# A hybrid SGU/SSD/MoE layer in one kernel: gain vectors multiplied into rows before the transposes, remainders taken out of PSUM banks

## The reference

```
h  = RMSNorm(x) * mix_norm
h @ w_in -> u | v | z | xBC (2048) | dt (16) | gate_a | gate_b
yA = gelu(u) * (W_s LayerNorm(gelu(v)) + b)            # 8 heads, 128 positions
xBC -> causal depthwise conv (4 taps) -> SiLU -> xs | B | C
yB = GroupedRMSNorm(SSD(xs, dt, B, C) * SiLU(z)) * ssm_norm
x += (sigmoid(gate_a) * (yA @ Wa) + sigmoid(gate_b) * (yB @ Wb)) @ Wo
x += MoE(RMSNorm(x))          # top 4 of 32 experts, clamped SwiGLU, w1 8 MB and w2 4 MB each
x += sigmoid((RMSNorm(x) * ple_norm) @ Wg) * (p @ Wp)
out = RMSNorm(x) * final_norm
```

## Time and profile before

| | |
|---|---|
| median of three runs | 1341.76 us |
| the profiled execution's own time | 1345.77 us |
| its span, first to last instruction | 1343.7 us |
| mean granted clock of PE | 0.965 of full speed |
| PE busy | 1240.8 us, 92% |
| DVE busy | 371.2 us, 28% |
| ACT busy | 238.3 us, 18% |
| POOL busy | 189.6 us, 14%, all of it before 302 us |
| DMA | 456.63 MB, mean 340 GB/s |

### The profile page before, as it was taken

The page is one execution under the profiler, slowest core; times in us unless marked ns, Lnnn a source line. Parts: engine busy times, 40 slices in busy tenths (PEclk is TensorE's granted clock), DMA queues, the critical chain, the costliest instruction groups (busy, mean ns, idle before and its releaser), DMA issues.

```text
span 1343.7 us, 15395 instructions
## 1 busy us (share of the span) xinstructions
PE 1240.8 (92%) x6309; PEld 657.5 (49%) x6309; DVE 371.2 (28%) x672; ACT 238.3 (18%) x284; POOL 189.6 (14%) x54
## 2 busy tenths in 40 slices
PE   1998999789899999999999999999999999999976
PEld 1996888667444444444333334333333433333342
DVE  6436731542212221122121112212111221211132
ACT  4454435432000010000010000001000000100011
POOL 6555557850000000000000000000000000000000
PEclk7988999899599999999999999999999999999988
DMA  6443347757199999999999999999999999999910
GB/s 212 157 130 125 123 168 247 300 172 278 43 410 429 429 429 429 429 428 427 428 429 428 429 429 429 429 429 429 427 429 428 429 428 429 429 429 429 429 53 31
DMA packets 61094, 456.63 MB, mean 340 GB/s; under 512 B 6784, under 2 KB 16368, under 8 KB 36496
## 3 DMA queue, kind: packets, MB, share of 16 engines
q1 hardware_dynamic: 61072, 456.32, 82.6%
HBM read 455.25 MB, written 1.05 MB: 340 GB/s over the span
## 4 chain that ended last, share of the span: by engine, by line
DMA 47%; PE 45%; DVE 4%; issue 1%; ACT 1%; SPq 0%; DVEq 0%; ACTq 0%
DMA wring<-in_w_dram 45%; PE bank L810 15%; PE bank L572 5%; PE bank L573 5%; PE bank L574 5%; PE bank L840 4%; PE bank L787 3%; DVE a_lo L1166 2%; PE bank L911 2%; PE bank L796 1%; DMA blk<-in_w_in_dram 1%; DMA blk<-in_w_branch_b_dram 1%; PE bank L675 1%; PE bank L859 1%; PE bank L697 1%
## 5 line engine op out<-in xcount | busy, mean ns | idle before, releaser
L810 PE MATMUL bank<-wring,hT 128*64 128x512 f32 x2048 | 456.0, 598 | 28.7 <-DMA wring<-in_w_dram 28.7
L810 PEld LDWEIGHTS bank<-wring,hT 128*64 128x64 f32 x2048 | 140.4, 137 | 322.9 <-issue 255.7
L840 PE MATMUL bank<-wring,xbcT 128*64 128x512 f32 x1024 | 226.8, 595 | 0.0
L538 POOL TENSOR_TENSOR blk_lo<-blk,blk_hi 128x2048 fp32r<-128x2048 f32 x40 | 187.2, 4690 | 111.2 <-ACT blk_hi L924 111.0
L1467 DVE TENSOR_SCALAR xbcT<-bank 128x512 f32<-128x512 f32 x32 | 22.1, 692 | 461.8 <-PE bank L816 461.8
L840 PEld LDWEIGHTS bank<-wring,xbcT 128*64 128x64 f32 x1024 | 70.8, 137 | 152.1 <-issue 152.1
L787 PEld LDWEIGHTS bank<-xbcT,ga 128*128 128x128 f32 x1056 | 126.2, 196 | 5.1 <-issue 2.3
L787 PE MATMUL bank<-xbcT,ga 128*128 128x64 f32 x1056 | 124.9, 278 | 1.8 <-issue 1.8
L1084 ACT ACTIVATE xbcT<-xbcT 128x512 f32<-128x512 f32 x32 | 20.2, 630 | 500.3 <-DVE xbcT L1467 500.3
L924 ACT ACTIVATE blk_hi<-blk 128x2048 fp32r<-128x2048 f32 x40 | 76.4, 1913 | 122.3 <-DMA blk<-in_w_in_dram 69.7
L572 PE MATMUL bank<-blk_hi,a_lo 128*128 128x512 f32 x192 | 78.1, 407 | 14.2 <-DVE a_lo L1166 8.7
(11 more groups left out here) (228 smaller groups left out, 970.1 us busy)
## 6 DMA issues: line engine op xcount, KB each, us to landing
wring<-in_w_dram SPq DMA_DIRECT2D x192, 2048.0 KB, 21.7
blk<-in_w_in_dram SPq DMA_DIRECT2D x28, 1024.0 KB, 5.2
blk<-in_w_branch_a_dram SPq DMA_DIRECT2D x4, 1024.0 KB, 5.3
blk<-in_w_branch_b_dram SPq DMA_DIRECT2D x4, 1024.0 KB, 6.4
blk<-in_w_out_dram SPq DMA_DIRECT2D x4, 1024.0 KB, 5.1
blk<-in_w_ple_gate_dram SPq DMA_DIRECT2D x4, 1024.0 KB, 8.9
x<-in_x_dram SPq DMA_DIRECT2D x4, 512.0 KB, 5.1
v<-in_w_ple_proj_dram SPq DMA_DIRECT2D x1, 1024.0 KB, 7.5
```

Source lines behind the costliest of these rows:

```text
L538: nc.gpsimd.tensor_tensor(dst, raw, hi.bitcast(FP32), ALU.subtract).then_inc(done, 1)
L810: last = mm(bank[dh * SLOTS:(dh + 1) * SLOTS, :], xgT[:, k, :], wring[:, 2 * c + kk, off + dh * W:off + (dh + 1) * W], start=(k == 0), sto ...
L840: last = mm(YB[dh * SLOTS:(dh + 1) * SLOTS, :], actT[:, kk * P + c * SLOTS:kk * P + (c + 1) * SLOTS], wring[:, at, (kk % 2) * D + dh * W:( ...
```

## The change

- `mix_norm` and `ssm_norm` are no longer rows to be transposed with the other parameters. Each is loaded as 1024 numbers on all 128 partitions: `mix_gain` (in z's buffer) right behind x, `ssm_gain` (in the upper part of the conv buffer) after the unit `("yo", 1)` is filled.
- DVE multiplies them into the rows, ahead of the transposes, in the instruction that multiplies with the root: two of 128x1024 at the start, eight of 128x256 for the SSD branch.
- The banks of `xT` and `ybT` then hold the finished values; high and low parts of both are taken straight from the banks, like those of `yaT` and `mT`. Two of the passes through SBUF, `hT` and `ybT`, are gone there.
- The second x tile's square sum is DVE's; a dummy root on ACT comes first.
- ACT splits block 0 after the high parts of `xT`, and in two halves of 128 columns of each k (`per_k`); POOL subtracts it in two halves and PE waits for each half.
- Half block 1 is loaded ahead of the parameter rows, and PE transposes these after the first xBC block.
- ACT splits the last half block of z before the exponentials of the decays. POOL still does all 40 subtractions; their semaphore is two (`xbc_low`, `nat_low`).

```diff
@@ -78,9 +78,9 @@
     nat = lambda n: [(n, b, t) for b in range(HALVES) for t in range(TT)]
-    u = [("param",)]
-    u += [("xT", t, h) for t, h in two]
-    u += [("xbc", b, j) for b in range(4) for j in range(2)]
+    u = [("xT", t, h) for t, h in two]
+    u += [("xbc", 0, 0), ("param",)]
+    u += [("xbc", b, j) for b in range(4) for j in range(2)][1:]
     u += [("dt",)]
...
@@ -106,8 +106,9 @@
 BANKS = 8
-ROWS = {"mix": 0, "ple": 8, "ssm": 16, "sgu_b": 24, "conv_b": 32, "conv_w": 48}
-NROWS = 48 + TAPS * CONV_TILES
+ROWS = {"ple": 0, "sgu_b": 8, "conv_b": 16, "conv_w": 32}
+NROWS = 32 + TAPS * CONV_TILES
+XBC_HALVES = 8
...
@@ -209,13 +210,14 @@
-        ybT = xbcT[:, 0:KT, :]
         wpp = flat(v).rearrange("p (k n) -> p k n", k=PLE // P)
         p_nat = xc[:, 2560:3072].rearrange("p (t n) -> p t n", t=TT)
+        ssm_gain = xc[:, 3072:4096].rearrange("p (g n) -> p g n", g=GROUPS)
+        mix_gain = z[:, 0, :]
         fnorm = z[:, 0, :]
...
@@ -420,13 +427,14 @@
                 load(x[:, t, :], x_in[0, t * P:(t + 1) * P, :], x_loaded[t])
+            load(mix_gain, vec(mix_norm), mix_loaded)
             load_half(0)
-            for key, src in (("mix", rows(mix_norm)), ("ple", rows(ple_norm)),
-                             ("ssm", rows(ssm_norm)), ("sgu_b", sgu_b[0]), ("conv_b", rows(conv_b)),
+            load_half(1)
+            for key, src in (("ple", rows(ple_norm)), ("sgu_b", sgu_b[0]), ("conv_b", rows(conv_b)),
                              ("conv_w", rows(conv_w[0]))):
                 load(prow[r:r + src.shape[0], :], src, rows_loaded)
-            for i in range(1, NB):
+            for i in range(2, NB):
                 load_half(i)
...
@@ -461,6 +469,7 @@
                     wait_filled(sp, ("yo", 1))
+                    load(ssm_gain.rearrange("p g n -> p (g n)"), vec(ssm_norm), ssm_loaded)
                     load(p_nat, p_in[0, 0].rearrange("(t p) n -> p t n", p=P), p_loaded)
...
@@ -538,12 +547,17 @@
-            for i in range(SPLIT):
-                if i == HALF_OF["xbc", 3, 0]:
+            for c in range(2):
+                cols = slice(c * P, (c + 1) * P)
+                pool.wait_ge(blk_high, c + 1)
+                subtract(per_k(blk_lo[:, 0, :])[:, :, cols], per_k(blk[:, 0, :])[:, :, cols], per_k(high(0))[:, :, cols],
+                         xbc_low)
+            for i in range(1, SPLIT):
+                if i == XBC_HALVES - 2:
                     pool.wait_ge(wdt_high, 1)
                     subtract(wdt_lo[:], wdt.rearrange("p k h -> p (k h)"), wdt_hi[:], wdt_low)
-                pool.wait_ge(blk_high, i + 1)
-                subtract(blk_lo[:, i % NB, :], blk[:, i % NB, :], high(i), blk_low)
+                pool.wait_ge(blk_high, i + 2)
+                subtract(blk_lo[:, i % NB, :], blk[:, i % NB, :], high(i), xbc_low if i < XBC_HALVES else nat_low)
...
@@ -581,7 +595,7 @@
-                        pe.wait_ge(blk_low, i + 1)
+                        pe.wait_ge(nat_low, i - XBC_HALVES + 1)
                         for t in range(TT):
...
@@ -595,29 +609,30 @@
             pe.wait_ge(consts, 1)
-            pe.wait_ge(rows_loaded, 16 * 6)
-            transposes(("param",), [prow[0:NROWS, :]])
             for t in range(TT):
-            pe.wait_ge(act_low, 4)
+            wait_taken(pe, *all_of("xT"))
             for b in range(4):
                     wait_empty(pe, name)
-
-                    pe.wait_ge(blk_low, i + 1)
                     for c in range(2):
+
+                        pe.wait_ge(xbc_low, i + 2 if i else c + 1)
                         for k in range(KT):
                     last.then_inc(full(name), 1)
+                    if i == 0:
+                        pe.wait_ge(rows_loaded, 16 * 4)
+                        transposes(("param",), [prow[0:NROWS, :]])
             pe.wait_ge(wdt_low, 1)
...
@@ -728,7 +743,7 @@
-            pe.wait_ge(act_low, 8)
+            wait_taken(pe, *all_of("ybT"))
             natural("wb", a_hi, a_lo)
...
@@ -921,7 +936,12 @@
                 act.wait_ge(blk_loaded[i % NB], 16 * (i // NB + 1))
-                fn(high(i), blk[:, i % NB, :], ACT.Copy).then_inc(blk_high, 1)
+                if i == 0:
+                    for c in range(2):
+                        cols = slice(c * P, (c + 1) * P)
+                        fn(per_k(high(i))[:, :, cols], per_k(blk[:, i, :])[:, :, cols], ACT.Copy).then_inc(blk_high, 1)
+                else:
+                    fn(high(i), blk[:, i % NB, :], ACT.Copy).then_inc(blk_high, 1)
...
@@ -932,7 +952,12 @@
-            square_sums(lambda t: act.wait_ge(x_loaded[t], 16), 0, u)
+            act.wait_ge(consts, 1)
+            fn(vmean[:, 0, 0:1], ones[:, 0:1], ACT.Sqrt)
+            act.wait_ge(x_loaded[0], 16)
+            fn(u[:, 0, :], x[:, 0, :], ACT.Square, accum_out=ssq[:, 0:1]).then_inc(ssq_done, 1)
+            act.wait_ge(ms_done, 1)
+            fn(rstd[:], ssq[:], ACT.Sqrt).then_inc(rstd_done, 1)
...
@@ -952,14 +977,19 @@
+            def high_parts(kind, dst):
+
+                for t in range(TT):
+                    for h in range(2):
+                        name = (kind, t, h)
+                        wait_filled(act, name)
+                        fn(dst[:, 4 * h:4 * h + 4, t * P:(t + 1) * P], seg4(bank_of(name)[:, :]),
+                           ACT.Copy).then_inc(act_high, 1)
+
+            act.wait_ge(xn_done, TT)
+            high_parts("xT", a_hi)
             split(0)
             split(1)
-
-            for t in range(TT):
-                for h in range(2):
-                    wait_taken(act, ("xT", t, h))
-                    cols = (slice(None), slice(4 * h, 4 * h + 4), slice(t * P, (t + 1) * P))
-                    fn(a_hi[cols], hT[cols], ACT.Copy).then_inc(act_high, 1)
             split(2)
...
@@ -995,15 +1025,6 @@
-            def high_parts(kind, dst):
-
-                for t in range(TT):
-                    for h in range(2):
-                        name = (kind, t, h)
-                        wait_filled(act, name)
-                        fn(dst[:, 4 * h:4 * h + 4, t * P:(t + 1) * P], seg4(bank_of(name)[:, :]),
-                           ACT.Copy).then_inc(act_high, 1)
-
             def copy(name, dst, src=None):
...
@@ -1018,6 +1039,7 @@
             natural("u", ACT.Gelu, u)
+            split(HALF_OF["z", 1, 1])
             for c in range(TT):
...
@@ -1025,7 +1047,10 @@
             for b in range(HALVES):
-                split_ahead("z", b)
+                if b == 0:
+                    split(HALF_OF["ga", 0, 0])
+                else:
+                    split_ahead("z", b)
                 for t in range(TT):
...
@@ -1051,12 +1076,7 @@
-            wait_filled(act, ("gb", 1, 1))
-            for t in range(TT):
-                for h in range(2):
-                    wait_taken(act, ("ybT", t, h))
-                    cols = (slice(None), slice(4 * h, 4 * h + 4), slice(t * P, (t + 1) * P))
-                    fn(a_hi[cols], ybT[cols], ACT.Copy).then_inc(act_high, 1)
+            high_parts("ybT", a_hi)
             split_ahead("wa", 1)
...
@@ -1147,29 +1167,27 @@
-            norm(0, v)
-            wait_filled(dve, ("param",))
-            cp(paramT[:], bank_of(("param",))[:, 0:NROWS]).then_inc(empty(("param",)), 1)
-            wait_taken(dve, ("param",))
-            for t in range(TT):
-                for h in range(2):
-                    scaled(("xT", t, h), hT, paramT[:, ROWS["mix"]:ROWS["mix"] + KT], t, h)
-
-            def low_parts(kind, raw, hi, lo, n):
+            def low_parts(kind, hi, lo, n):
                         cols = (slice(None), slice(4 * h, 4 * h + 4), slice(t * P, (t + 1) * P))
-                        if raw is not None:
-                            tt(lo[cols], raw[cols], hi[cols].bitcast(FP32), ALU.subtract).then_inc(act_low, 1)
-                        else:
-                            name = (kind, t, h)
-                            tt(lo[cols], seg4(bank_of(name)[:, :]), hi[cols].bitcast(FP32),
-                               ALU.subtract).then_inc(empty(name), 1)
-
-            low_parts("xT", hT, a_hi, a_lo, 0)
+                        name = (kind, t, h)
+                        tt(lo[cols], seg4(bank_of(name)[:, :]), hi[cols].bitcast(FP32),
+                           ALU.subtract).then_inc(empty(name), 1)
+
+            dve.wait_ge(x_loaded[1], 16)
+            stt(u[:, 1, :], x[:, 1, :], 1.0, x[:, 1, :], ALU.mult, ALU.mult, accum_out=ssq[:, 1:2]).then_inc(ssq_done, 1)
+            norm(0, None)
+            dve.wait_ge(mix_loaded, 16)
+            for t in range(TT):
+                stt(v[:, t, :], x[:, t, :], rstd[:, t:t + 1], mix_gain, ALU.mult, ALU.mult).then_inc(xn_done, 1)
+            low_parts("xT", a_hi, a_lo, 0)
+            wait_filled(dve, ("param",))
+            cp(paramT[:], bank_of(("param",))[:, 0:NROWS]).then_inc(empty(("param",)), 1)
+            wait_taken(dve, ("param",))
...
@@ -1343,11 +1361,14 @@
             dve.wait_ge(yrstd_done, 1)
```

(24 more changed lines are left out.)

## The result

The changed kernel took 1320.47 us (median of four runs, 1319.52 to 1320.76), the kernel before 1341.28 (four runs). The ratio is 0.9842, 95% interval 0.9825 to 0.9859: 20.8 us, against a forecast of 25.8 and a time of 1316.0 within 1311 to 1324. The profiled execution took 1319.52 us, with a span of 1317.5.

A forecast was written before the change was run, and what follows sets the result against it. PE's two waits for `a_lo` were taken to bound the kernel ahead of the DMA-paced expert loop. Terms of 14.7 and 11.1 us sum to 25.8, giving 1316.0 us from the 1341.8 median, range 1311 to 1324.

The forecast's parts named there:

- first term: Start of the kernel: PE's first xBC block begins at 16.3 instead of 31.34 us, saving 14.7 us, range 10.0 to 17.0.
- A wait for `a_lo` is POOL's hold on DVE; a bank read is free of it: Low parts at both waits: about 5 us each beside GpSimd from SBUF, 2.48 us for four out of a PSUM bank.
- POOL next in line, but just covered: First blocks: GpSimd works just ahead of PE without delaying it, by 0.9 us at the tightest.
- Second term: Between "wa" and "wb": PE's 8.7 us wait for ybT's low parts and 2.4 of low clock go, 11.1 us.
- taken from both: The 25.8 us saving subtracted alike from the profiled execution, 1345.8 to 1320.0, and from the median, 1341.8 to 1316.0.
- Nothing given back by the additions: Behind "wb": DVE's additions of ga and gb end as far behind it as before, so nothing is lost.
- Edits at no time: z's last half split earlier and eight ssm multiplications, 3.6 us for 2.36: both off PE's path, no time.
- Loop moves one for one: Expert loop: its DMA stream shifts by whatever starts expert 0 earlier, with 29.37 us per expert unchanged.
- PE waited for POOL at no block but the first: Rival, 10%: GpSimd binds the first blocks at the start, giving 1322 us.
- its matmuls reached full pace: Rival, 4%: PE's clock stays at its low level through the first eight blocks, up to 45 us longer, 1361 us.
- "wb" had its weights: Rival, 8%: the weights of "wb" come late, so PE's second wait stays with another owner, 1327 us.
- the multiplications with the ssm row ended before POOL's next subtraction: Rival, 4%: DVE's ssm-row multiplications are caught by GpSimd's subtractions and delay "wa", 1322.4 us.

The follow-up runs named there:

- pool_wait: Kernel before plus one wait: GpSimd begins its weight subtractions only when the four low parts of xT are done; 1330.93 us, ratio 0.991.
- order_both: Kernel before plus two waits: GpSimd's first subtraction waits for xT's low parts, its first of wb for ybT's; 1324.70 us, ratio 0.9879.
- ybt_only: Kernel before with only the ybT part changed: ssm gain row, eight multiplications, high and low parts from the banks; 1333.67 us, ratio 0.9933.
- split_first: Kernel after, but ACT splits the first half of block 0 ahead of xT's high parts; 1318.77 us, ratio 0.9823.
- the second trace: Kernel before, unchanged, profiled once more in the first experiment; 1338.91 us, span 1336.9.
- start_only: Kernel after with the ybT part as in the kernel before, so only the start is changed; 1326.93 us, ratio 0.988.
- after_again: Kernel after, unchanged, run again beside the kernel before on one chip; 1320.35 us, ratio 0.9843.
- order_gap: Kernel before plus one wait: GpSimd's subtraction of wb's third quarter waits for the low parts of ybT; 1340.34 us, ratio 0.9993.
- whole_block: Kernel after with block 0 split and subtracted whole instead of in halves; 1322.63 us, ratio 0.9855.
- the run with 21: split_first plus 21 extra PE matmuls of 128 columns between constants at the start; 1317.26 us, ratio 0.9826.
- the run with 44: split_first plus 44 extra PE matmuls of 128 columns between constants at the start; 1321.05 us.

## Why the prediction was right, and where it was off

The forecast was a saving of 25.8 us; 20.8 came, with the time inside the range. The mechanism held at every step; the sizes of both terms were too large, the first by 1.5 us, the second by about 4 for a typical execution. The forecast for an execution like the profiled one, 1320.0, met 1319.5, and that is in part luck: the 1.5 us that the first term lacks came back behind "wb", mostly as scatter in the expert loop.

- **A wait for `a_lo` is POOL's hold on DVE; a bank read is free of it.** Right, and shown four ways: pool_wait and order_both (POOL away: 0.6 us each), ybt_only (both forms in one execution), split_first (bank reads through a subtraction).
- **First term, 14.7.** It measured 13.7 at the first block, 13.2 at dt and 12.9 at the end of "wa". The multiplications started at 8.37, not 7.3: the gain row, 6.6 us on its way, landed at 8.3 us, between the 7.0 taken and the 9.1 of the bound. ACT's high parts came 0.85 apart, at the pace of PE's transposes (four at 0.21 to 0.23), with 0.60 each instead of 0.52. Halves cost half (2.36 and 1.0), as taken. PE's first block begins at 17.61, outside the 16 to 17 named as a sign, and takes 7.8 us, 0.5 more than before.
- **POOL next in line, but just covered.** Right: five pieces back to back from 15.11 to 33.5, and no wait of PE for POOL once block 0 has begun. One sign of being wrong, over 2 us of PE waiting for POOL in the first blocks, came by its words: PE waits 4.2 us ahead of block 0. But the forecast's own layout had 4.0 there (transposes until 12.3, start at 16.3), so the sign should have named the waits behind that one. The parameter transpose cost 0.3 or less.
- **Second term, 11.1.** "wb" ends 24.1 us earlier than in the profiled trace, 11.2 more than "wa" does: near exact for that execution. It is the step that failed for the median, together with the line "taken from both". The prediction saw that its execution was 4.0 us above the median, and subtracted the whole of its wait from the median all the same. The wait is 8.7 in some executions and 4.3 in others, so the typical term is about 7. Against the second trace the same stages give 12.7 + 7.3 = 20.0 at the end of "wb", and start_only's median is 6.6 above after's. The hint was in the rows: a low part of 0.68 among ones of 5 us says that a gap let one through, and this gap depends on a load.
- **Nothing given back by the additions.** Right: the last of them ends at 272.3, 6.7 us behind "wb"; before it was 7.0 (291.85 + 4.79 against 289.67).
- **Edits at no time.** z's half: 1.4 us of waiting on DVE, 0.1 on the kernel. The ssm multiplications: 3.26 us (3.6 taken), done 1.0 us before POOL's next subtraction at 197.19.
- **Loop moves one for one.** Right: 24.7 at expert 0, 26.2 at the end, with 980.5 against 982.0 us for the loop, inside its own scatter. One expert still takes 29.37 us where DMA bounds it (606.64 to 636.01 in the chain of waits).

Of the rivals, none came: PE waited for POOL at no block but the first, its matmuls reached full pace 4.4 us into block 0 (0.21 us apart before that, 0.12 after, against 3.5 us in the kernel before), "wb" had its weights, and the multiplications with the ssm row ended before POOL's next subtraction.

## What to carry to other kernels

Where VectorE and GpSimd both stream SBUF data, look for VectorE instructions of two SBUF tensors whose length is that of a GpSimd instruction; let one operand come from PSUM, or let GpSimd wait: two semaphore waits alone gave 16 of the 21 us here. A wait that ends with another engine's instruction comes in whole instructions, so before subtracting it from a median, get a second trace or look whether a gap of a fraction of a microsecond decides it. And when a start is a chain, try each piece that an engine could do while idle: half a split put ahead of the high parts was worth about 1.5 us.

## What the runs showed that I had not expected

- The kernel before had two lengths of one wait, 4.3 and 8.7 us: long where POOL's pause was 0.57 or 0.89 us, short where it was 1.19 or 1.67. Its 39 runs spread over 10.5 us, the five of after_again over 2.0. This race between a load and the low parts is one cause of that spread, not the only one: kernels without it also spread, order_gap over 4.6 us in 12 runs, order_both over 6.1 in six, whole_block over 6.1 in six.

> The kernel after, unchanged, beside before and the others on one chip, for its distance to them. Theory: the saving against the median of before is 20 to 23 us, with runs of after within 2 us of each other while those of before spread over 8 or more.

1320.35 us (1318.38 to 1320.37), ratio 0.9843 (0.9821 to 0.9864); 20.7 us under before, whose 17 runs beside it spread over 7.7, just under the 8 expected.

- A float32 matmul of 128 columns between constants counts as two in the trace (x88 for 44). On average it took 0.34 us in the run with 21 (7.21 us) and 0.26 in the run with 44 (11.61 us), so the length of such a row of extra matmuls is better set from a trace than from a count.
